# Prologue of an attention block kernel: raw memory rows transposed, norm weights as scales of the copies from PSUM, and a place of its own for every x row and memory weight tile

## What is computed

```python
def rmsnorm(x, g):                       # x (.., 1024), g (1024,)
    xf = x * rsqrt(mean(x * x, axis=-1, keepdims=True) + 1e-6)
    return xf * g

hn   = rmsnorm(x, g_norm)                # x (1024, 1024)
proj = hn @ w_in                         # w_in (1024, 4352): q, k, v, gate of heads A, B, M
memn = rmsnorm(mem, g_mem)               # mem (256, 1024)
kv   = memn @ w_mem_kv                   # w_mem_kv (1024, 1024): keys and values of the memory
...                                      # A: windowed attention, B: differential, M: over kv
y    = rmsnorm(x + gated @ w_out, g_final)
```

## Time and profile before

| | us |
|---|---|
| median of 3 runs (730.59 to 730.65) | 730.63 |
| the profiled execution | 732.36 |
| its span, first to last instruction | 730.5 |
| first matmul of a memory tile | 17.26 |
| head start | 77.77 |

### The profile page before, as it was taken

How to read it: one execution, slowest core, us unless ns; L and a number is a source line. 1 busy time by engine, 2 the same in 40 slices (tenths; PEclk the granted TensorE clock), 3 DMA queues, 4 the chain that set the end, 5 groups by cost and what they waited for, 6 DMA issues and landing times.

```text
span 730.5 us, 11970 instructions
## 1 busy us (share of the span) xinstructions
PE 712.9 (98%) x3908; PEld 595.5 (82%) x3908; DVE 428.6 (59%) x919; ACT 311.9 (43%) x720; POOL 227.7 (31%) x201
## 2 busy tenths in 40 slices
PE   8999999999999999999999999999999898999996
PEld 7888788888888888888888888888888786888885
DVE  5884335776773567677367777636767586422231
ACT  5771333454543345454344536334453543212210
POOL 3564132324423233442322334233243501311210
PEclk9999999999999999999999999999999999999999
DMA  8662121111033111104210110421140278513111
GB/s 267 201 190 70 29 59 31 30 30 31 1 121 81 29 29 29 29 0 134 68 29 29 29 29 0 144 59 30 30 119 3 61 161 220 179 58 122 66 64 42
DMA packets 79527, 53.55 MB, mean 73 GB/s; under 512 B 36224, under 2 KB 72064, under 8 KB 79488
## 3 DMA queue, kind: packets, MB, share of 16 engines
q1 hardware_dynamic: 79488, 53.10, 26.0%
HBM read 44.18 MB, written 8.91 MB: 73 GB/s over the span
## 4 chain that ended last, share of the span: by engine, by line
PE 87%; issue 4%; DVE 3%; POOL 3%; ACT 1%; DMA 1%; SPq 0%; DVEq 0%; POOLq 0%; ACTq 0%
PE acc L1305 17%; PE acc L1306 17%; PE acc L1307 17%; PE score L1305 3%; PE score L1306 3%; PE score L1307 3%; PE score L1433 3%; PE trans L1306 3%; PE trans L1305 3%; PE score L1435 3%; PE trans L1307 3%; PE trans L1454 2%; POOL w_lo L809 2%; PE score L1511 2%; PE mixo L1306 2%
## 5 line engine op out<-in xcount | busy, mean ns | idle before, releaser
L1305 PE MATMUL acc<-x_hi,w_hi 128*128 128x512 f32 x544 | 216.7, 398 | 0.1
L1306 PE MATMUL acc<-x_lo,w_hi 128*128 128x512 f32 x544 | 212.9, 391 | 0.0
L1307 PE MATMUL acc<-x_hi,w_lo 128*128 128x512 f32 x544 | 212.6, 391 | 0.0
L809 POOL TENSOR_TENSOR w_lo<-w_raw,w_hi 128x512 fp32r<-128x512 f32 x86 | 113.1, 1337 | 191.3 <-ACT w_hi L549 191.3
L1307 PEld LDWEIGHTS acc<-x_hi,w_lo 128*128 128x128 f32 x544 | 102.4, 188 | 22.3
L1305 PEld LDWEIGHTS acc<-x_hi,w_hi 128*128 128x128 f32 x544 | 102.7, 189 | 21.2 <-issue 1.8
L1306 PEld LDWEIGHTS acc<-x_lo,w_hi 128*128 128x128 f32 x544 | 102.7, 189 | 18.4
L666 ACT ACTIVATE logits<-logits,stats_b 128x256 f32<-128x256 f32 (+3 forms) x64 | 52.6, 824 | 46.8 <-DVE stats_b L1110 46.8
L1102 DVE CUSTOM_DVE_ANT_0 logits<-score,b_bias 128x512 f32<-128x512 f32 (+1 forms) x96 | 53.8, 599 | 22.1 <-PE score L1435 19.2
L549 ACT ACTIVATE w_hi<-w_raw 128x512 fp32r<-128x512 f32 x86 | 49.4, 624 | 28.5 <-PE acc L1307 20.0
L675 ACT ACTIVATE p_hi<-trans 128x512 fp32r<-128x512 f32 x56 | 32.5, 595 | 63.2 <-PE trans L1454 38.9
(11 more groups left out here) (190 smaller groups left out, 1335.2 us busy)
## 6 DMA issues: line engine op xcount, KB each, us to landing
w_raw<-in_w_in SPq DMA_DIRECT2D x68, 256.0 KB, 3.3
wo_raw<-in_w_out SPq DMA_DIRECT2D x22, 256.0 KB, 7.1
mixed<-gates SPq DMA_DIRECT2D x9, 512.0 KB, 4.3
mix_raw<-mixed SPq DMA_DIRECT2D x8, 576.0 KB, 6.1
w_raw<-in_w_mem_kv SPq DMA_DIRECT2D x16, 256.0 KB, 3.8
logits<-in_x SPq DMA_DIRECT2D x8, 512.0 KB, 4.8
x_res<-in_x SPq DMA_DIRECT2D x8, 512.0 KB, 3.3
out_y<-y_row SPq DMA_DIRECT2D x16, 256.0 KB, 2.1
```

The source lines that it names most:

```text
L809: last = pool.tensor_tensor(w_lo[:, slot, cols], w_raw[:, slot, cols], w_hi[:, slot, cols].bitcast(F32), ALU.subtract)
L1305: pe.matmul(out, a_hi, b_hi, start=start, stop=False, skip_group_check=True)
L1306: pe.matmul(out, a_hi, b_lo, start=False, stop=False, skip_group_check=True)
L1307: return pe.matmul(out, a_lo, b_hi, start=False, stop=stop, skip_group_check=True)
```

## The change

- **Memory rows** are transposed raw. The two tiles of memory rows go into four banks of PSUM (`spread_mem`), two pieces of 128x256 in each. The norm weight of a column is now a number for each partition of the transposed piece, and comes in as the `scale` of ACT's copy (`take_bank_hi`) and as the scalar of DVE's multiply and subtract (`take_bank_lo`). rstd of the memory rows is applied last: DVE spreads it over 256 columns, PE transposes that, and DVE multiplies each memory tile's product by it (`mem_tile`, where a plain copy was).
- **Norm weights** come as 16 rows of 128 numbers, are turned by one transpose, and stand as 16 columns in `gain_cols`. The two copies of 512 KB are gone, and with them the need of `gates` for them.
- **x rows** are still multiplied by rstd ahead of the transpose, but by rstd alone, in place, and in pairs: `normalise(pair)` makes two rstd in one chain of six tiny instructions and scales two rows. Each of the 8 rows has its own home.
- **Memory weights**: tiles 2 to 7 have homes in places that are used only later, so SP waits for nothing until tile 8.
- **Halves**: PE starts a tile when its first low half is made (`w_lo_half`) and waits for the second one at its middle. DVE makes the very first low half. Transposes rotate over four banks, memory tiles over four accumulators. The loops of the prologue are written out.
- PE's work without a use is 14 transposes, 2 and 8 wide matmuls.
- PE takes the transposes of the x rows later: pair 0 begins behind memory tile 3, and pairs 2 and 3 end between the halves of tiles 8 and 9. Three DVE instructions on bias tables go from the end of the prologue to its start.

```diff
-BUSY = (32, ((0, 512), (8, 512), (16, 512), (32, 512)), ((64, 512), (0, 516), (0, 576)))
+BUSY = (14, 2, 8)
...
+        x_raw = [logits[:, 0, 0, :], logits[:, 0, 1, :], logits[:, 1, 0, :], logits[:, 1, 1, :],
+                 gates["a"], gates["b"], v_rows[0][:, :], v_rows[1][:, :]]
...
             sp.dma_start(mem_raw[0][:, :], mem_rows[:, 0, :]).then_inc(mem_full[0], 16)
-            sp.dma_start(g_mem_b[:, :], g_mem.partition_broadcast(P)[:, 0, :]).then_inc(gmem_full, 16)
+            sp.wait_ge(gain_zeroed, 1)
+            for n, g in enumerate((g_norm, g_mem)):
+                sp.dma_start(gain_rows[n * KT:(n + 1) * KT, :], g.rearrange("l (k p) -> (l k) p", p=P))\
+                  .then_inc(gain_full, 16)
             sp.dma_start(mem_raw[1][:, :], mem_rows[:, 1, :]).then_inc(mem_full[1], 16)
...
+            for n in range(3):
+                load_mem_tile(n)
+            for t in range(5):
+                load_row(t)
+                load_mem_tile(t + 3)
+            load_row(5)
...
+            def take_bank_hi(n, out, gain):
+
+                act.wait_ge(t_full, n + 1)
+                for j in range(2):
+                    last = act.activation(out(j), pre_t[n][:, j * 2 * P:(j + 1) * 2 * P], ACT.Copy, scale=gain(j))
+                last.then_inc(t_hi, 1)
...
+            for n in range(PRE_TILES):
+                if n > 0:
+                    pre_lo_half(n, 0).then_inc(w_lo_half, 1)
+                pre_lo_half(n, 1).then_inc(w_lo_done, 1)
...
+            def normalise(pair):
+
+                fine2 = pair_rstd(pair + 1)
+                for n in range(2):
+                    row = x_raw[2 * pair + n]
+                    last = dve.tensor_scalar(row, row, fine2[:, n:n + 1], None, ALU.mult)
+                last.then_inc(rows_done, 1)
...
+            def mem_tile(n):
+
+                dve.wait_ge(acc_full, n + 1)
+                out = mk_raw[:, n // 2, :] if n % 2 == 0 else mv_t[:, (n // 2) * MEM:(n // 2 + 1) * MEM]
+                dve.tensor_tensor(out, pre_acc[n % 4][:, 0:MEM], mem_rstd, ALU.mult).then_inc(acc_free, 1)
...
+            for n in range(MEM_TILES):
+                mem_tile(n)
+                if n == 1:
+                    pe.wait_ge(gain_made, 1)
+                    pe.wait_ge(mem_spread_made, 1)
+                    for par in range(2):
+                        last = pe.transpose(mixo[:, par * P:(par + 1) * P], mem_spread[:, par, :], ident[:, :])
+                    last.then_inc(mem_rstd_turned, 1)
+                if n >= 3:
+                    pair, half = divmod(n - 3, 2)
+                    for b in range(2 * half, 2 * half + 2):
+                        spread_rows(pair, b)
```

More of the change, by code:

```diff
@@ L597, in _ @@
-            with act.Fori(0, 3) as q:
-                for par in range(2):
-                    prologue_step(q, par)
-            prologue_step(3, 0)
-            prologue_step(3, 1, more=False)
-            act.wait_ge(table_step, 2)
+            row_squares(mem_raw[0][:, :], 0, mem_full[0])
+            mem_bank_hi(0)
+            w_hi_half(0, 0)
+            mem_bank_hi(1)
+            w_hi_half(0, 1)
+            mem_bank_hi(2)
+            mem_bank_hi(3)
+            split_hi(1)
+            row_squares(mem_raw[1][:, :], 1, mem_full[1])
@@ new lines, in _ @@
+            row_squares(x_raw[4], 6, rows_full[4])
+            split_hi(7)
+            for b in range(2):
+                x_bank_hi(1, b)
+            row_squares(x_raw[5], 7, rows_full[5])
+            pair_std(3)
+            split_hi(8)
+            row_squares(x_raw[6], 8, rows_full[6])
+            for b in range(2, 4):
+                x_bank_hi(1, b)
+            split_hi(9)
+            row_squares(x_raw[7], 9, rows_full[7])
+            pair_std(4)
+            for pair in (2, 3):
+                for b in range(4):
+                    x_bank_hi(pair, b)
@@ L975, in _ @@
-            with dve.Fori(0, 3) as q:
-                for par in range(2):
-                    prologue_step(q, par)
-            prologue_step(3, 0)
-            prologue_step(3, 1, more=False)
+            dve.wait_ge(const_made, 5)
+            table(dve.tensor_scalar(a_bias[CHUNK:P, :, :, :], a_bias[CHUNK:P, :, :, :], float(CHUNK), None, ALU.add))
+            table(dve.scalar_tensor_tensor(out=b_bias[:, :], in0=b_bias[:, :], scalar=-1.0, in1=b_bias[:, :],
+                                           op0=ALU.mult, op1=ALU.min))
@@ new lines, in normalise, with take_bank_lo @@
+            def normalise(pair):
[4 more added lines that the diff above has]
+                last.then_inc(rows_done, 1)
+            def take_bank_lo(n, hi, out, gain):
+                dve.wait_ge(t_hi, n + 1)
+                for j in range(2):
+                    last = dve.scalar_tensor_tensor(out=out(j), in0=pre_t[n][:, j * 2 * P:(j + 1) * 2 * P],
+                                                    scalar=gain(j), in1=hi(j).bitcast(F32), op0=ALU.mult,
+                                                    op1=ALU.subtract)
+                last.then_inc(t_free, 1)
@@ new lines, in _ @@
+            dve.wait_ge(gain_made, 1)
+            mem_bank_lo(0)
+            dve.wait_ge(w_hi_done, 1)
+            dve.tensor_tensor(w_lo[:, 0, 0:HALF], w_raw[:, 0, 0:HALF], w_hi[:, 0, 0:HALF].bitcast(F32), ALU.subtract)\
+               .then_inc(w_lo_first, 1)
+            for b in range(1, 4):
+                mem_bank_lo(b)
+            fine = pair_rstd(0)
+            dve.tensor_copy(mem_spread, fine.rearrange("p (a n) -> p a n", n=1).broadcast_to([P, 2, P]))\
+               .then_inc(mem_spread_made, 1)
@@ new lines, in mem_tile @@
+            def mem_tile(n):
+                if n >= 4:
+                    pe.wait_ge(acc_free, n - 3)
+                for k in range(KT):
+                    if k == 0:
+                        pe.wait_ge(*((w_lo_half, n) if n else (w_lo_first, 1)))
+                    if k == KT // 2:
+                        pe.wait_ge(w_lo_done, n + 1)
+                    if n == 0 and k % 2 == 0:
+                        pe.wait_ge(t_free, k // 2 + 1)
+                    w = slice(k * P, (k + 1) * P)
+                    last = product(pre_acc[n % 4][:, 0:MEM], w_hi[:, n % 2, w], w_lo[:, n % 2, w], mem_hi[:, k, :],
+                                   mem_lo[:, k, :], k == 0, k == KT - 1)
+                last.then_inc(acc_full, 1)
@@ new lines, in _ @@
+            shared_half(8, 0, first)
+            shared_half(8, 0, rest)
+            for b in range(2, 4):
+                spread_rows(2, b)
+            shared_half(9, 0, first)
+            for b in range(2):
+                spread_rows(3, b)
+            shared_half(9, 0, rest)
+            for b in range(2, 4):
+                spread_rows(3, b)
+            shared_half(8, 1, first)
+            for v in range(2):
+                pe.wait_ge(t_free, 17 + v)
+                for b in range(4):
+                    last = pe.transpose(pre_t[20 + v][:, b * P:(b + 1) * P],
+                                        mv_t[:, (4 * v + b) * P:(4 * v + b + 1) * P], ident[:, :])
+                last.then_inc(t_full, 1)
@@ L1390, in head @@
+            shared_half(8, 1, rest)
+            pe.wait_ge(const_made, 6)
+            for v in range(2):
+                spread_shared(v)
+            shared_half(9, 1, first)
+            shared_half(9, 1, rest)
+            pe.wait_ge(acc_free, 11)
+            for v in range(2, 4):
+                spread_shared(v)
             def head(h, order):
```

403 lines of the change are left out of this document (227 added, 176 removed).

## The result

The change makes the kernel slower: 736.14 us median (734.93 to 736.88, 5 executions) against 730.65 (730.59 to 732.12), a ratio of 1.0067 (95% interval 1.0051 to 1.0083). Forecast were 725.4, with 0.05 for slower. The profiled execution took 736.88, its span is 735.1. All times in this text are of executions in the chip's usual state; one execution of e2, at 789.81 us and a mean granted clock of 0.85, is left out.

The account below looks back on a forecast made before the run. PE bounds the kernel, busy in 98% of the span. Head start: 67.4 + 0.4 + 0.8 + 0.6 + 3.3 = 72.5 against 77.77, 5.2 us won, so 730.63 - 5.2 = 725.4, range 721.4 to 728.6.

Parts of the forecast that it names:

- The start: Memory tiles 0 and 1: first matmul near 9.6, packed start at 10.0 in place of 17.26, 7.2 us won.
- 8.2 at the latest: Start of the kernel: the first weights land as third transfer by 8.2 us.
- The spreading: Memory rstd, behind tile 1: PE waits 0.6 us for DVE's L1091, between 0 and 1.2.
- near 16.0 on POOL's border: Memory rstd chain on DVE: it ends near 16.0 us; PE is through with tile 1 at 16.4.
- Pairs: Ahead of the x-row transposes: DVE held by POOL's low halves, PE waits 1.9, 0.7 and 0.7 us for pairs 0, 1, 2.
- A long wait costs the clock too: Rival at pair 0's wait: one clock fall, 1.7 us lost, giving 727.1; chance 0.22, shared with late loads.
- The work between: Prologue up to the head start: 57.1 us of PE work carried over, 0.3 for two transposes, 0.8 for switches.
- the change touches nothing there: Behind the head start: the same 652.2 us to the end, PE busy 641.91 of 652.23.
- Late loads: Rival in the memory tiles: queued loads land 1 to 2 us late, 727.0 to 729.2; chance 0.22, shared with the clock fall.
- The clock stays low at the start: Rival at the first tiles: filler cut from 60 to 24 instructions keeps 1.2 GHz, 736 with four tiles; chance 0.05.
- DVE is not held: Rival at the x-row pairs: pair 0 costs 0.4, the others nothing; head start 69.0, time 721.9; chance 0.18.
- the right collision: Prologue: DVE's chain and scalings stand until POOL's current low half is through, 3.3 us over the pairs, 0.6 for spreading.

Follow-up runs that it names:

- e2: Changed kernel plus 12 wide matmuls on zeros ahead of PE's wait for the memory rstd spreading and 12 ahead of pair 0's: 732.70 us, ratio 1.0035.
- e1: Changed kernel with POOL's low halves of tiles 2, 4, 6, 8 waiting for DVE's memory rstd spreading and x-row pairs 0, 1, 2: 724.90 us, ratio 0.9918.
- e6: Changed kernel with POOL's low halves waiting for DVE's spreading and row pairs, and gain_cols in idle columns of small: 720.65 us, ratio 0.9866.
- e5: Changed kernel with gain_cols put into idle columns of small, so no tensor behind it shifts by 64 bytes: 733.38 us, ratio 1.0030.
- e7: Kernel before, with 64 bytes left free ahead of stats_b, where gain_cols stands in the changed kernel: 732.82 us, ratio 1.0024.
- e3: Changed kernel with each two-column step of the rstd chain written as two one-column TENSOR_SCALARs, scalings unchanged: 729.20 us, ratio 0.9957.
- e10: Kernel before, with 64 bytes left free behind x_lo, ahead of logits: 734.38 us, ratio 1.0040.

## Why the prediction was wrong

The profiled execution was to take 727.1 and took 736.88: 9.8 us more. 9.1 of them lie ahead of the head start (72.5 forecast, 81.57 measured), 0.8 behind it.

- **The start: right in kind, 1.0 us short.** The first memory matmul came at 10.56 in place of some 9.6, and tile 1 at 14.44 in place of 13.4. The second memory rows landed at 7.36 (6.6 forecast) and the weights at 9.14, where "8.2 at the latest" was forecast. Of the 0.9 us, 0.8 came with the second load, 3.2 us behind the first; the third came 1.8 behind the second. The landing is not the same in every execution: 8.80 for the weights in e1, 8.55 in e2. The gain at the start was real, and e6 keeps it.
- **The spreading: 3.0 us short, the step that failed first.** It was taken as 0.6, between 0 and 1.2, because only L1091 itself was weighed; the chain was let through to "near 16.0 on POOL's border". The earlier trace rows had shown a step held and the next, bigger one held behind it. Applied to each step here that gives four of the five held ones, the three with two tensor inputs and the spreading, one low half each. The fifth, L1027, is a multiply and add of constants on two columns, for which no row of before had a price. The chain ended at 19.66.
- **Pairs: right place, 3.8 us short.** 1.9 + 0.7 + 0.7 were reckoned, 4.36 + 1.40 + 1.38 measured. For pair 0, two steps (L1035, L1037) and both scalings were held, where the working had two multiplies held and the scalings, at 0.7 each, free behind POOL's end. It counted the two low halves of one turn. Those of the next follow as soon as PE is through with tile 3 (29.69), and met the scalings (3.50 for two, 1.42 free); DVE and POOL there:

```profile
27.78 1.23 DVE L1035 TENSOR_TENSOR m_probs<-m_probs 128x2 f32<-128x2 f32 x1
29.04 1.22 DVE L1037 TENSOR_SCALAR m_probs<-m_probs 128x2 f32<-128x2 f32 x1
...
30.50 3.50 DVE L1048 TENSOR_SCALAR logits<-logits,m_probs 128x1024 f32<-128x1024 f32 x2
```

```profile
27.68 2.56 POOL L899 TENSOR_TENSOR w_lo<-x_raw_hi,w_hi 128x512 fp32r<-128x512 f32 x2 [6.83 <-ACT w_hi L598]
30.50 2.95 POOL L899 TENSOR_TENSOR w_lo<-x_raw_hi,w_hi 128x512 fp32r<-128x512 f32 x2 [0.27 <-ACT w_hi L598]
```

For pairs 1 and 2 the chain went as worked, with two steps held (1.23 and 1.24 us for pair 1) and the scalings free (1.42 for two). Most of the 0.7 us more is there because PE asked earlier, 3.7 us behind the end of the tile and not 4.15.

- **The clock: a rival that came true, and not as an alternative.** "A long wait costs the clock too" was priced at one fall of 1.7 us, beside a wait of 1.9. With waits of 3.62 and 4.36 there were two falls. From the start of tile 1 to the head start e1 has 53.99 us (from 14.09), 1.47 of them waits, so 52.5 of work at clock 1.00; after has 67.13 (from 14.44), 10.76 of them waits, so 56.4. The falls cost 3.9 us by this, 3.7 by e2. The wait and the fall belong to one case and should have been added up: the forecast's own mechanism, a little larger, brings the rival's price with it.
- **The work between: 2.7 us too long.** 55.2 us were reckoned from tile 1 to the head start without waits, 52.5 are shown. The busy time of the earlier trace rows was carried over and 0.8 for switches put on top. The traces show where it went: eight transposes and the switches around them had taken 1.18 us before (38.07 to 39.25), and in e1 they take 0.80 (28.59 to 29.39), so the switches by banks of four cost nothing, and each of the eight rows gave 0.4 us. That is more than the 2.7; what took some of it back was not taken apart.

```profile
28.59 0.60 PE L1464 MATMUL score<-ident,logits 128*128 128x128 f32 x4
29.03 0.60 PE L1464 MATMUL mixo<-ident,logits 128*128 128x128 f32 x4
29.39 0.36 PE L1443 MATMUL acc<-q_b,w_hi 128*128 128x256 f32 x1
```

- Together, with the rounding: 1.0 + 3.0 + 3.8 + 3.9 - 2.7 = 9.1.
- **The heads: "the change touches nothing there" was the second step that failed.** It moved `x_hi` and `x_lo` by 64 bytes, at 2.2 us (e5, e7). One line of the diff, an allocation, was read as free; the odd paddings beside it were a hint that went unweighed. In the profiled execution 1.4 us came back, as the clock did not fall behind the wait of 2.10.
- **The other rivals.** Late loads fall: from the first memory matmul to the heads no wait of PE names one. "The clock stays low at the start", from the cut filler, gave almost the right time, 736, by a mechanism that did not occur: the granted clock was 0.99 to 1.00 up to 20 us. That the time came out near 736 is luck for this rival. "DVE is not held" is what e1 makes true, but for one step; 69.0 for the head start was forecast for it, 68.08 measured.
- The Trainium skill ("SBUF — State Buffer", "SBUF: two separate sides") has the exclusive lock, with a float32 copy within SBUF among the instructions that it stops. The trace agrees: L1091 took 1.32 us beside a low half and 0.29 without. So the copy cost the upper end of the range taken, 1.2; the larger part of the miss lay in the chain ahead of it.

In short: the change moves a chain of small DVE steps into the stretch where POOL has most to do, and PE stands behind it. Forecast was the right collision, priced at 3.9 us of waits; it cost 10.8, and 3.7 to 3.9 more by the clock. Four waits on POOL and 64 bytes turn 736.1 into 720.65, 1.3% below the kernel before.

## What to carry to other kernels

When DVE and POOL share a stretch, price a chain of small DVE steps step by step: each with two tensor inputs in SBUF, or with two or more columns of a multiply, cost as much here as POOL's instruction beside it, however small it was. The engine with slack should be the one that waits, by a semaphore, and a one-column form is the other way out. A wait of PE can cost more than itself, for the clock may fall behind it (here behind some of 2.10 us, and behind 2.85, 3.62 and 4.36); cheap work in it gives that back. And compare the address of every tensor before and after: a new one in the middle of the list is a change to all behind it, so put it at the end or into idle columns.

## What the runs showed of the hardware that was not expected

- A multiply and add of constants on **two** columns is held by POOL (L1027 1.08 us, L1037 1.22). On **one** column it was not: in e3 two such take 0.21 us together while a low half runs. A reciprocal of two columns was not held either (0.17 us at 14.67 in e3). Of the small steps beside POOL, has only a tensor_tensor of one column, held.
- A two-column one ran in 0.17 us (L1037 at 18.20) when POOL stood between two halves for 0.19 us, so a gap as short as that is enough for a step to get through.
- 64 bytes between the places of the two operands cost 4 to 6 ns for each k tile of the projections, 2.2 to 2.5 us in 507; between those of the output projection they cost 2% of its pace, 2.7 us. 512 bytes cost nothing. What within those 512 bytes decides, and by which mechanism, stays open.
- Behind one and the same wait of 2.10 us the granted clock fell in some executions and not in others of the same kernel: sixteen of 27, by the two groups of times and by their mean clocks. Twelve of the traces of this case have that wait; in five the clock fell behind it, and seven show no fall. In a trace where it fell, the rest of the kernel takes 148.2 to 148.4 us (150.9 in e10), and 146.2 to 147.2 where it did not. Behind waits of 2.85 us and more it fell in every trace shown; behind those of 1.79 us and less, in none.
